# Second MLP products of three chunks as two interleaved groups of seven half-size products, with two of the side sums on GpSimd and six raw weight buffers

## The chip, the cores and the metric

The kernel runs on one core of a Trainium2 chip. The metric is the device time of one execution in microseconds. Before the change the median of 3 runs is 793.33 us (792.94 to 793.57).

## What is computed

One layer of a streaming encoder for 544 tokens (512 prompt frames, 32 sample frames), feature dimension 1024, all float32. The part that matters here is the MLP; its hidden width is 4096 and is worked off in four chunks of 1024:

```python
x = x + merged @ w_out
x = x + jnp.square(jax.nn.relu(rms_norm(x, g_mlp) @ w_up)) @ w_down
x = x + jax.nn.sigmoid(rms_norm(x, g_ple) @ w_ple_gate) * (p[layer] @ w_ple_proj)
```

Before it come the input projection, a pooling mixer and stick-breaking attention, behind it the gate of the last line ("ple") and the final norm. None of these is touched except where they share the weight buffers.

## The kernel before

**Precision.** Every float32 operand is split in a high part (fp32r, made by ScalarE) and a low part (the difference, made by VectorE). A product is three matmuls: high by high, high by low, low by high, each over 272 columns (half the tokens).

**Weights.** Weights come as tiles of 128x1024 (512 KB). SyncE loads a raw tile into one of 10 raw buffers (`RAW_BUFS`, line 84: two in `raw`, eight in `raw_more`), ScalarE makes `w_hi` from it (`hi`, line 699), VectorE makes `w_lo` (`ahead`, line 1456), in a ring of four split tiles (`W_RING`). Both engines make tile t+3 at the step of tile t; ScalarE's `hi` waits until TensorE has finished tile t-1 (semaphore `full`), whose ring place it takes. SyncE fills a raw buffer again when the low part of the tile before in it is made (`wait_free`, line 525; `wlo_done`). It issues strictly in the order of `STAGED_LOADS`.

**First products of a chunk (up).** Each chunk has two groups (g even, g odd; 512 hidden features each). A group is a Winograd form of Strassen's product: seven half-size products in the order A11, S1, S2, S4, S3, A12, A22 of the weight side (`SIDES`, line 71), of 24 matmuls each (`product_of`, line 1352), against seven token-side operands `u_hi`, `u_lo` that lie ready. The weight sides are S1 = A21+A22, S2 = A11+S1, S3 = A21+A11, S4 = A12+S2 in the stored tiles (signs are in the stored weights and operands). Each of the four sums is a second DMA that adds into the raw buffer (`second_part`, line 654, issued by GpSimd, `accum_op=ALU.add`): for S1 and S3 from HBM, for S2 and S4 from another raw buffer. So a group has 7 loads and 4 adding DMAs.

Results accumulate in PSUM (four slots of two banks; an even group has slots 0 and 1, an odd one 2 and 3). ScalarE copies the first three results out to `h_of` (`copy_quarter`, line 933), VectorE adds three more there (`add_quarter`, line 1793) and scales by the inverse norm and clips (`scaled_second`, lines 1817 and 1822; `scaled_first`, line 1803). ScalarE squares (`hidden_hi`, lines 948 and 949) into `b_hi` and in place, VectorE makes `b_lo` (`hidden_lo`, line 1828). `h_of` is single: the next group's first copy waits until the low part of the first half is made.

**Second products of a chunk (down).** Eight dense products of 48 matmuls each (`down`, line 1373, matmuls on lines 1061, 1064 and 1067), from 8 loads, PSUM slots in turn; the first two are interleaved by hidden features so that late features are used last. VectorE adds each result to the residual `xt` (`add_residual`, line 1742). In the last chunk VectorE and ScalarE also build the operands of the ple gate between them.

**GpSimd** only issues the adding DMAs in the MLP. Earlier, in the attention stage, it runs masks (line 634) and the window sums of the pooling mixer (`window_sums`, line 614), while VectorE splits weights (line 1448) and attention operands (lines 1549, 1644).

## Time and profile before

| | |
|---|---|
| median of 3 runs | 793.33 us (792.94 to 793.57) |
| profiled execution | 793.77 us, span 791.9 us |
| granted TensorE clock, mean | 0.996 |
| TensorE busy | 773.7 us (98%) |
| VectorE busy | 494.8 us (62%) |
| ScalarE busy | 381.5 us (48%) |
| GpSimd busy | 96.9 us (12%) |
| DMA moved | 110.18 MB, 139 GB/s mean |
| MLP, from the first up product to the ple gate | 357.99 to 719.98 us of the span |

The span is that of the slowest (here only) core from first to last instruction; the time reported for the same execution is 1.9 us more. PE is TensorE (matmul), PEld its weight load, DVE VectorE, ACT ScalarE, POOL GpSimd, SP SyncE; SPq and POOLq are their DMA issues. Matmuls are pipelined: each is shown as 288 ns long, but successive ones start about 125 ns apart, so busy time and count say more than the mean duration.

### The profile page before, as it was taken

Reading aid. Unit: us, or ns where it says so; the run is one execution under the profiler, and the core shown is the slowest. Engines: PE = TensorE matmul, PEld = TensorE weight load, DVE = VectorE, ACT = ScalarE, POOL = GpSimd, SP = SyncE. Lnnn points to the kernel's source line nnn. Section 1 sums busy time; section 2 is a strip of 40 time slices with the busy share of each in tenths; the row PEclk is TensorE's granted clock in tenths of the full one; section 3 lists DMA queues with packets and bytes.
Section 4 is the critical chain, followed back from the end, with each engine's and each line's share of the span. In section 5 each row is a group of like instructions: output and inputs, shape, how many; then the busy total and the mean of one; then the engine's idle time right before and its main releaser. Section 6 shows DMA issues by size and latency. Waiting matters only on the chain.

```text
span 791.9 us, 14329 instructions
## 1 busy us (share of the span) xinstructions
PE 773.7 (98%) x6050; PEld 765.2 (97%) x6050; DVE 494.8 (62%) x606; ACT 381.5 (48%) x443; POOL 96.9 (12%) x169
## 2 busy tenths in 40 slices
PE   8899999999999999999999999999999999999993
PEld 8899999999999899999999999999999999999993
DVE  5876566566566547787763367434763367677965
ACT  6554534535575443665641255213642155555643
POOL 1040140150150000020001100020001100100001
PEclk9999999999999999999999999999999999999998
DMA  7342231232221316786566847587575856826402
GB/s 236 99 125 74 70 120 53 82 105 56 98 90 55 107 54 206 240 202 178 179 171 168 202 160 206 139 188 183 158 192 145 204 171 180 195 82 161 119 1 113
DMA packets 33097, 110.18 MB, mean 139 GB/s; under 512 B 4496, under 2 KB 4496, under 8 KB 33040
## 3 DMA queue, kind: packets, MB, share of 16 engines
q1 hardware_dynamic: 24768, 84.72, 32.4%
q0 software_dynamic: 6016, 21.04, 14.9%
q10 hardware_dynamic: 2256, 3.60, 1.3%
q8 instruction: 44, 0.72, 0.4%
q14 instruction: 13, 0.11, 0.0%
HBM read 94.33 MB, written 4.52 MB: 125 GB/s over the span
## 4 chain that ended last, share of the span: by engine, by line
PE 90%; DVE 5%; ACT 2%; issue 1%; DMA 1%; SPq 1%; DVEq 0%; ACTq 0%
PE psum L1352 24%; PE psum L1061 19%; PE psum L1067 19%; PE psum L1064 19%; PE psum L1114 1%; DMA xt<-x_t 1%; PE psum L1042 1%; PE psum L1142 1%; PE psum L1043 1%; PE psum L1044 1%; PE psum L1140 1%; PE psum L1430 1%; PE psum L1102 1%; DVE work L1473 1%; PE psum L1101 1%
## 5 line engine op out<-in xcount | busy, mean ns | idle before, releaser
L699 ACT ACTIVATE w_hi<-raw_more 128x1024 fp32r<-128x1024 f32 x84 | 88.7, 1056 | 133.0 <-PE psum L1067 100.7
L1064 PE MATMUL psum<-b_lo,w_hi 128*128 128x272 f32 x688 | 142.0, 288 | 0.0
L1061 PE MATMUL psum<-b_hi,w_hi 128*128 128x272 f32 x672 | 139.3, 288 | 0.0
L1067 PE MATMUL psum<-b_hi,w_lo 128*128 128x272 f32 x672 | 138.8, 288 | 0.0
L1061 PE MATMUL psum<-a_hi,w_hi 128*128 128x272 f32 x576 | 120.8, 291 | 3.3 <-DVE a_lo L1462 1.2
L1456 DVE TENSOR_TENSOR w_lo<-raw_more,w_hi 128x1024 fp32r<-128x1024 f32 x84 | 102.2, 1222 | 34.6 <-ACT w_hi L699 34.3
L1067 PE MATMUL psum<-a_hi,w_lo 128*128 128x272 f32 x576 | 119.0, 288 | 0.0
L1064 PE MATMUL psum<-a_lo,w_hi 128*128 128x272 f32 x576 | 118.8, 288 | 0.0
L1352 PE MATMUL psum<-u_hi,w_hi 128*128 128x272 f32 x560 | 115.9, 288 | 0.2 <-ACT h_of L933 0.2
L1352 PE MATMUL psum<-u_hi,w_lo 128*128 128x272 f32 x560 | 115.7, 288 | 0.0
L1352 PE MATMUL psum<-u_lo,w_hi 128*128 128x272 f32 x560 | 115.5, 287 | 0.0
L1064 PEld LDWEIGHTS psum<-b_lo,w_hi 128*128 128x128 f32 x688 | 108.1, 188 | 0.0
L1061 PEld LDWEIGHTS psum<-b_hi,w_hi 128*128 128x128 f32 x672 | 105.4, 188 | 0.8 <-issue 0.7
L1067 PEld LDWEIGHTS psum<-b_hi,w_lo 128*128 128x128 f32 x672 | 105.1, 189 | 0.0
L1061 PEld LDWEIGHTS psum<-a_hi,w_hi 128*128 128x128 f32 x576 | 90.2, 188 | 4.4 <-DVE a_lo L1462 2.0
L1064 PEld LDWEIGHTS psum<-a_lo,w_hi 128*128 128x128 f32 x576 | 90.5, 189 | 0.0
L1067 PEld LDWEIGHTS psum<-a_hi,w_lo 128*128 128x128 f32 x576 | 90.0, 189 | 0.0
L1352 PEld LDWEIGHTS psum<-u_hi,w_hi 128*128 128x128 f32 x560 | 87.9, 188 | 0.5 <-issue 0.4
L1352 PEld LDWEIGHTS psum<-u_lo,w_hi 128*128 128x128 f32 x560 | 88.3, 188 | 0.0
L1352 PEld LDWEIGHTS psum<-u_hi,w_lo 128*128 128x128 f32 x560 | 87.5, 188 | 0.0
L1742 DVE TENSOR_TENSOR xt<-psum,xt 128x544 f32<-128x544 f32 x40 | 28.9, 723 | 88.2 <-PE psum L1067 88.2
L1448 DVE TENSOR_TENSOR w_lo<-raw,w_hi 128x1024 fp32r<-128x1024 f32 x41 | 51.8, 1265 | 41.5 <-ACT w_hi L691 41.3
(245 smaller groups left out, 1010.3 us busy)
## 6 DMA issues: line engine op xcount, KB each, us to landing
raw_more<-w_tiles SPq DMA_DIRECT2D x84, 512.0 KB, 4.3
raw<-w_tiles SPq DMA_DIRECT2D x66, 512.0 KB, 3.5
raw_more<-w_tiles POOLq DMA_DIRECT2D x16, 512.0 KB, 6.7
raw_more<-raw_more POOLq DMA_DIRECT2D x14, 512.0 KB, 8.3
xt<-x_t SPq DMA_DIRECT2D x8, 272.0 KB, 6.2
y_t<-xt SPq DMA_DIRECT2D x8, 272.0 KB, 2.5
raw<-w_tiles POOLq DMA_DIRECT2D x4, 512.0 KB, 7.6
raw_more<-raw POOLq DMA_DIRECT2D x3, 512.0 KB, 6.4
```

Source lines behind the costliest of these rows:

```text
L699: act.activation(w_hi[:, t % W_RING, :, :].rearrange("p k c -> p (k c)"), src, ACT.Copy)\
L1042: pe.matmul(out, hi, rhi, start=first, stop=False, skip_group_check=True)
L1043: pe.matmul(out, hi, rlo, start=False, stop=False, skip_group_check=True)
L1044: return pe.matmul(out, lo, rhi, start=False, stop=last, skip_group_check=True)
L1061: pe.matmul(base[:, h, :], w_hi[:, s, wk, :], at(hi, k, h * HALF, (h + 1) * HALF), start=(opens and q == 0), stop=False, skip_group_check= ...
L1064: pe.matmul(base[:, h, :], w_hi[:, s, wk, :], at(lo, k, h * HALF, (h + 1) * HALF), start=False, stop=False, skip_group_check=True)
L1067: mm = pe.matmul(base[:, h, :], w_lo[:, s, wk, :], at(hi, k, h * HALF, (h + 1) * HALF), start=False, stop=(closes and q == len(ks) - 1), s ...
L1101: pe.matmul(z, b_lo[:, keys], b_hi[:, both], start=(b != 3), stop=False, skip_group_check=True)
L1352: mm = pe.matmul(out[:, two, :], w_part[:, t % W_RING, 2 * k + two, :], u_part[:, op, k, :], start=(OPENS[s] and k == 0 and w_part is w_hi ...
L1448: dve.tensor_tensor(w_lo[:, s, :, :].rearrange("p k c -> p (k c)"), raw[:, t % RAW_RING, :], w_hi[:, s, :, :].rearrange("p k c -> p (k c)" ...
L1456: dve.tensor_tensor(w_lo[:, t % W_RING, :, :].rearrange("p k c -> p (k c)"), src, w_hi[:, t % W_RING, :, :].rearrange("p k c -> p (k c)"), ...
L1742: dve.tensor_tensor(halves(xt[:, m, :]), slot(n), halves(xt[:, m, :]), ALU.add).then_inc(taken, 1)
```

## The change

In chunks 0, 1 and 2 the second products take the same seven-product form as the first ones. The outputs are split in two sets e = 0, 1 (four of the eight output tiles each), and the 14 products of 24 matmuls run in the order (side, e) = (A11,0), (A11,1), (S1,0), (S1,1), ... The token side is now seven sums of quarters of the hidden features (B11, B21, B22, T3, NT1, NT2, T4), each split in high and low: VectorE makes NT1, T3, NT2 and T4 (`operand_sum`) and all seven low parts (`operand_low`), ScalarE the high parts (`square_hi`, `sum_hi`). They are made by group of hidden features, in the steps around the start of the next group. A product uses hidden features of both groups; for the first two products the part of the even group of both comes first. Chunk 3 stays dense. The first products of all chunks keep their seven products.

In all groups, S2 and S4 are no longer DMAs: GpSimd adds 128x1024 tiles in place, S2 in the buffer of A11 once A11's low part is made, S4 in the buffer of S1 once S1's low part is made. A group has 5 loads and 2 adding DMAs. There are 6 raw buffers in place of 10.

```diff
-LOADS = SIDES
-ADDED = {"S1": ("A21", "A22"), "S2": ("A11", "S1"), "S3": ("A21", "A11"), "S4": ("A12", "S2")}
+LOADS = ("S1", "A11", "A12", "S3", "A22")
+DN_LOADS = ("A11", "S1", "A12", "S3", "A22")
+ADDED = {"S1": ("A21", "A22"), "S3": ("A21", "A11")}
+LIES_IN = {"S2": "A11", "S4": "S1"}
-RAW_BUFS = 10
+RAW_BUFS = 6
```

The order of the loads (`staged_loads`):

```diff
+        if c < SEVENS:
+            seq.extend((DN_GROUPS + 2 * c + e, what) for what in DN_LOADS for e in range(2))
+        else:
+            seq.extend(("down", c, q) for q in range(KT))
```

SyncE, what a load waits for (`wait_free`):

```diff
-                        if what in ("S1", "S2"):
-                            sp.wait_ge((s2_in if what == "S1" else s4_in)[g % 2], 16 * (g // 2 + 1))
-                        sp.wait_ge(wlo_done, t_group(g, SIDES.index(what)) + 1)
+                        if what == "A11":
+                            sp.wait_ge(s4_made, nth_group(g) + 1)
+                        last = {"A11": "S2", "S1": "S4"}.get(what, what)
+                        sp.wait_ge(wlo_done, group_tile(g, last) + 1)
```

GpSimd:

```diff
+            def sum_two(g):
+
+                pool.wait_ge(*side_ready(g, "S1"))
+                pool.wait_ge(wlo_done, group_tile(g, "A11") + 1)
+                a = side_buf(g, "S2")
+                pool.tensor_tensor(a, a, side_buf(g, "S1"), ALU.add).then_inc(s2_made, 1)
+
+            def sum_four(g):
+
+                pool.wait_ge(s2_made, nth_group(g) + 1)
+                pool.wait_ge(*side_ready(g, "A12"))
+                pool.wait_ge(wlo_done, group_tile(g, "S1") + 1)
+                pool.tensor_tensor(side_buf(g, "S4"), side_buf(g, "S2"), side_buf(g, "A12"), ALU.add)\
+                    .then_inc(s4_made, 1)
+
+            def sums_of(g):
+                second_part(g, "S1")
+                second_part(g, "S3")
+                sum_two(g)
+                sum_four(g)
 
             for c in range(CHUNKS):
-                for g, what in ((0, "S1"), (0, "S2"), (1, "S1"), (0, "S4"), (0, "S3"), (1, "S2"), (1, "S3"), (1, "S4")):
-                    second_part(2 * c + g, what)
+                sums_of(2 * c)
+                sums_of(2 * c + 1)
+                if c < SEVENS:
+                    two = (DN_GROUPS + 2 * c, DN_GROUPS + 2 * c + 1)
+                    for g in two:
+                        second_part(g, "S1")
+                    for g in two:
+                        sum_two(g)
+                    for g in two:
+                        sum_four(g)
+                    for g in two:
+                        second_part(g, "S3")
```

ScalarE:

```diff
+            def square_hi(g, name):
+
+                act.activation(two_tiles(operand(0, name, g % 2)), hidden(name), ACT.Square).then_inc(ohi_done, 1)
+                for of in ("B11", "B12") if name == "B11" else (name,):
+                    act.activation(hidden(of), hidden(of), ACT.Square).then_inc(ohi_done, 1)
+
+            def sum_hi(g, name):
+
+                act.wait_ge(sum_done, nth_t(g, name))
+                act.activation(two_tiles(operand(0, name, g % 2)), hidden(name), ACT.Copy).then_inc(ohi_done, 1)
...
+            def up_seven(g):
+
+                for s in range(T_UP):
+                    n = NTH[("up", g, s)]
+                    if s == 0 and g % 2 == 1:
+                        last_quarter_hi(g - 1)
+                        sum_hi(g - 1, "NT1")
+                    ahead(TILE[("up", g, s)])
+                    if s == 0 and g % 2 == 1:
+                        sum_hi(g - 1, "T3")
...
+                    if g and s == 0:
+                        act.wait_ge(olo_done, nth_lo(g - 1, "NT1"))
+                        act.wait_ge(sum_done, nth_t(g - 1, "NT2"))
...
+                    if BY_ACT[s]:
+                        copy_quarter(g, n, s)
```

TensorE:

```diff
+            def down_seven(c):
+
+
+                for from_group in range(2):
+                    for e in range(2):
+                        if from_group == 0:
+                            weights(TILE[("dn", c, 0, e)])
+                            place_for(NTH[("dn", c, 0, e)])
+                        if e == 0:
+                            pe.wait_ge(olo_done, nth_lo(2 * c + from_group, "B11"))
+                        mm = second_product(c, 0, e, from_group)
+                        if from_group == 1:
+                            mm.then_inc(full, 1)
+                for s in range(1, T_UP):
+                    for e in range(2):
+                        weights(TILE[("dn", c, s, e)])
+                        place_for(NTH[("dn", c, s, e)])
+                        if e == 0:
+                            pe.wait_ge(olo_done, nth_lo(2 * c + 1, NAME[OPERAND[s]]))
+                        second_product(c, s, e, 0)
+                        second_product(c, s, e, 1).then_inc(full, 1)
```

VectorE:

```diff
+            def operand_low(g, name):
+
+                dve.wait_ge(ohi_done, nth_hi(g, ("sq " if name[0] == "B" else "hi ") + name))
+                dve.tensor_tensor(two_tiles(operand(1, name, g % 2)), hidden(name),
+                                  two_tiles(operand(0, name, g % 2)), ALU.subtract).then_inc(olo_done, 1)
...
+            def up_seven(g):
+                for s in range(T_UP):
+                    if s == 0 and g % 2 == 1:
+                        scaled_second(g - 1, "A22")
+                        operand_low(g - 1, "B11")
+                        operand_sum(g - 1, "NT1")
+                        operand_low(g - 1, "B21")
+                        operand_sum(g - 1, "T3")
+                        operand_low(g - 1, "NT1")
+                        operand_sum(g - 1, "NT2")
+                    ahead(TILE[("up", g, s)])
+                    if s == 0 and g % 2 == 1:
+                        operand_sum(g - 1, "T4")
+                        operand_low(g - 1, "NT2")
+                        operand_low(g - 1, "T3")
+                    if s == 1 and g % 2 == 1:
+                        operand_low(g - 1, "T4")
+                    if s == 5:
+                        operand_low(g, "B22")
+                    group_step(g, s)
...
+            def down_seven(c):
+                g = 2 * c + 1
+                for j in range(2 * T_UP):
+                    if j == 0:
+                        scaled_second(g, "A22")
+                        operand_low(g, "B11")
+                        operand_sum(g, "NT1")
+                        operand_low(g, "B21")
+                        operand_sum(g, "T3")
+                        operand_low(g, "NT1")
+                        operand_sum(g, "NT2")
+                    ahead(TILE[("dn", c, j // 2, j % 2)])
+                    if j == 0:
+                        operand_sum(g, "T4")
+                        operand_low(g, "NT2")
+                    if j == 1:
+                        operand_low(g, "T3")
+                        operand_low(g, "T4")
+                    second_taken(c, j // 2, j % 2)
```

`group_step` is the old body of `up_group` (`add_quarter`, `scaled_second` of S3, `scaled_first`). `second_taken` adds or subtracts a result in PSUM to or from a quarter of `xt` (544 elements), 14 times in a chunk in place of 8 `add_residual`.

## Rows read from the trace of the kernel before

**Rows 1.** The page, busy time by engine, the whole span.
```profile
PE 773.7 (98%) x6050; PEld 765.2 (97%) x6050; DVE 494.8 (62%) x606; ACT 381.5 (48%) x443; POOL 96.9 (12%) x169
```

**Rows 2.** Windows: one chunk's up part, then its down part; columns in the first line.
```profile
core 0: us, PE busy (x) PEld busy (x) DVE busy (x) ACT busy (x) POOL busy (x), PEclk, DMA share, GB/s
...
449.50:491.60 42.10, 42.10 (x338) 42.10 (x338) 28.67 (x28) 22.69 (x25) 0.87 (x1) 1.00 0.61 180
491.60:539.70 48.10, 48.10 (x386) 48.10 (x385) 18.06 (x19) 11.74 (x12) 6.12 (x7) 1.00 0.70 173
```

**Rows 3.** The chain that ended last, in order of time: start, length, what.
```profile
357.99 9.05 PE psum L1352 x72
...
449.48 42.07 PE psum L1352 x336
539.66 42.05 PE psum L1352 x336
```

**Rows 4.** Groups by line and form, VectorE and ScalarE: count, busy us, mean ns.
```profile
L1742 DVE TENSOR_TENSOR xt<-psum,xt 128x544 f32<-128x544 f32 x40 | 28.9, 723 | 88.2 <-PE psum L1067 88.2
...
L699 ACT ACTIVATE w_hi<-raw_more 128x1024 fp32r<-128x1024 f32 x84 | 88.7, 1056 | 133.0 <-PE psum L1067 100.7 <-PE psum L1352 30.1 <-PE psum L1044 2.1
...
L715 ACT ACTIVATE ev<-xt 128x544 f32<-128x544 f32 x28 | 17.8, 647 | 2.4 <-DVE work L1473 1.0 <-DVE work L1470 0.9 <-issue 0.5
...
L933 ACT ACTIVATE h_of<-psum 128x544 f32<-128x544 f32 x27 | 16.8, 622 | 24.8 <-PE psum L1352 19.0 <-DVE b_lo L1828 5.8
```

**Rows 5.** Timeline where a chunk's up part ends: start, length, instruction [idle before].
```profile
486.41 0.73 DVE L1817 SCALAR_TENSOR_TENSOR h_of<-h_of,rn 128x544 f32<-128x544 f32 x1
487.06 1.22 DVE L1456 TENSOR_TENSOR w_lo<-raw_more,w_hi 128x1024 fp32r<-128x1024 f32 x1
488.66 0.72 DVE L1793 TENSOR_TENSOR h_of<-h_of,psum 128x544 f32<-128x544 f32 x1 [0.38 <-PE psum L1352]
489.41 1.29 DVE L1803 SCALAR_TENSOR_TENSOR h_of<-h_of,rn 128x1088 f32<-128x1088 f32 x1
490.62 1.22 DVE L1456 TENSOR_TENSOR w_lo<-raw,w_hi 128x1024 fp32r<-128x1024 f32 x1
...
491.39 0.41 PE L1061 MATMUL psum<-b_hi,w_hi 128*128 128x272 f32 x2
...
494.10 0.72 DVE L1822 SCALAR_TENSOR_TENSOR h_of<-psum,rn 128x544 f32<-128x544 f32 x1
```

**Rows 6.** Line 1549, its instructions in ns, min/median/max.
```profile
L1549 DVE TENSOR_TENSOR later_lo<-later,later_hi x8: 546/552/1751, 48.8 to 252.0; 128x384 fp32r<-128x384 f32 x8
```

**Rows 7.** Timeline of the attention stage, VectorE beside GpSimd's additions.
```profile
101.11 1.75 DVE L1549 TENSOR_TENSOR later_lo<-later,later_hi 128x384 fp32r<-128x384 f32 x1
101.28 1.16 POOL L614 TENSOR_TENSOR gates<-upad 128x573 f32<-128x573 f32 x1
102.52 1.35 POOL L614 TENSOR_TENSOR gates<-gates 128x571 f32<-128x571 f32 x1
102.79 0.68 DVE L1644 TENSOR_TENSOR b_hi<-psum,b_hi 128x512 fp32r<-128x512 f32 x1
103.39 1.56 DVE L1448 TENSOR_TENSOR w_lo<-raw,w_hi 128x1024 fp32r<-128x1024 f32 x1
```

**Rows 8.** Line 1456, all splits of staged tiles from `raw_more`, ns.
```profile
L1456 DVE TENSOR_TENSOR w_lo<-raw_more,w_hi x84: 1215/1224/1228, 341.8 to 761.5; 128x1024 fp32r<-128x1024 f32 x84
```

**Rows 9.** GpSimd's additions, lines 614 and 625, ns, min/median/max.
```profile
L614 POOL TENSOR_TENSOR gates<-upad x4: 1153/1157/1172, 46.2 to 218.1; 128x573 f32<-128x573 f32 x4
...
L625 POOL TENSOR_TENSOR gates<-gates,invc x4: 185/334/459, 57.4 to 226.0; 128x2 f32<-128x2 f32 x1, 128x4 f32<-128x4 f32 x1, 128x8 f32<-128x8 f32 x1, 128x16 f32<-128x16 f32 x1
```

**Rows 10.** DMA issues: count, KB each, median us to landing; last line: line 663 alone.
```profile
raw_more<-w_tiles SPq DMA_DIRECT2D x84, 512.0 KB, 4.3
...
raw_more<-w_tiles POOLq DMA_DIRECT2D x16, 512.0 KB, 6.7
raw_more<-raw_more POOLq DMA_DIRECT2D x14, 512.0 KB, 8.3
...
DMA to landing us min/median/max: 4.5/7.1/12.4
```

More of the change, by code:

```diff
@@ L1390, in down, with second_product @@
                     dense(slot(n), t % W_RING, ALL, B).then_inc(full, 1)
+            NAME = {B11: "B11", NT1: "NT1", NT2: "NT2", B22: "B22", T3: "T3", B21: "B21", T4: "T4"}
+            def second_product(c, s, e, from_group):
+                t, name = TILE[("dn", c, s, e)], NAME[OPERAND[s]]
+                out = slot(NTH[("dn", c, s, e)])
+                hi, lo = (operand(part, name, from_group) for part in range(2))
+                for i in range(2):
+                    k = 2 * from_group + i
+                    for w_part, h_part in ((w_hi, hi), (w_hi, lo), (w_lo, hi)):
+                        for two in range(2):
+                            mm = pe.matmul(out[:, two, :], w_part[:, t % W_RING, 2 * k + two, :],
+                                           h_part[:, i * HALF:(i + 1) * HALF],
+                                           start=(OPENS[s] and k == 0 and w_part is w_hi and h_part is hi),
+                                           stop=(k == KT // 2 - 1 and w_part is w_lo), skip_group_check=True)
+                return mm
@@ new lines, in operand_sum @@
+            def operand_sum(g, name):
+                first, second = {"NT1": ("B11", "B12"), "T3": ("B22", "B12"), "NT2": ("B22", "NT1"),
+                                 "T4": ("NT2", "B21")}[name]
+                over = {"NT1": "B11", "NT2": "B22", "T4": "B21"}.get(name)
+                if over:
+                    dve.wait_ge(olo_done, nth_lo(g, over))
+                if name == "NT1":
+                    dve.wait_ge(ohi_done, nth_hi(g, "sq B12"))
+                if name != "NT1":
+                    dve.wait_ge(sum_done, nth_t(g, T_ORDER[T_ORDER.index(name) - 1]))
+                if name in ("NT1", "T3"):
+                    ins = dve.tensor_tensor(hidden(name), hidden(first), hidden(second), ALU.subtract)
+                else:
+                    ins = dve.scalar_tensor_tensor(out=hidden(name), in0=hidden(first), scalar=-1.0,
+                                                   in1=hidden(second), op0=ALU.mult, op1=ALU.subtract)
+                ins.then_inc(sum_done, 1)
@@ L1831, in statistics, with second_taken @@
+            def second_taken(c, s, e):
+                n, side = NTH[("dn", c, s, e)], SIDES[s]
+                x = x_quarter(side, e)
+                earlier = {"S4": "S2", "S3": "S1", "A12": "A11"}.get(side)
+                if earlier:
+                    dve.wait_ge(taken, taken_count(NTH[("dn", c, SIDES.index(earlier), e)]))
+                dve.wait_ge(full, n + 1)
+                dve.tensor_tensor(x, x, slot(n), ALU.subtract if X_QUARTER[side][0] else ALU.add).then_inc(taken, 1)
             def statistics(name):
@@ L1886, in _ @@
                 for s in range(T_UP):
-                    ahead(t_ple(g, s))
+                    ahead(TILE[("ple", g, s)])
                     if s == 3 and g == 0:
```

307 lines of the change are left out of this document (202 added, 105 removed).

## The prediction

> **What bounds the kernel now.** The page's busy times come first: TensorE is busy 98% of the span, VectorE 62%, ScalarE 48% [rows 1]. Then the windows: in a chunk TensorE is busy for all 42.10 us of the up part and all 48.10 us of the down part at full granted clock, while VectorE works 28.67 and 18.06 us [rows 2]. The chain in order of time says the same: a chunk's 336 up matmuls are one unbroken piece of 42.07 us, and the next chunk's piece starts 90.18 us after the last one's [rows 3]. So a matmul costs 42.07/336 = 0.1252 us, and 720 of them are 90.15 us: a chunk is TensorE's work and nothing else. Fewer matmuls shorten it as long as VectorE, ScalarE, GpSimd and the loads keep inside it.
>
> **What goes.** A down part falls from 8x48 = 384 to 14x24 = 336 matmuls: 48x0.1252 = 6.01 us a chunk, **18.0 us** for three. The new chunk is 84.1 us of matmuls, and a product lasts 3.005 us. The bound from below is thus 793.8 - 18.0 = 775.8.
>
> **What comes, and its price.** VectorE: a split 1.22 us [rows 8], an operation on 544 elements 0.72 [rows 4], `scaled_first` 1.29. In the timeline the next operation starts 0.08 us before the last one's end if it doesn't need its result (489.41 to 490.62 for one of 1.29), else 0.03 after it (488.66 to 489.41 for 0.72) [rows 5]. So I count 1.14 or 1.25, 0.64 or 0.75, 1.21. ScalarE: a split 1.06, 544 elements 0.65 from SBUF and 0.62 from PSUM [rows 4]. A chunk's VectorE work becomes 28 splits, 14 `second_taken`, and twice 16 operations on 544 and a `scaled_first`: 28x1.22 + 46x0.72 + 2x1.29 = 70 us of 84. It fits, but not evenly: the operands of a group fall within 15 us around the start of the next one.
>
> GpSimd's sums: no row shows one of 1024 elements. A 573-element addition takes 1.15 us and a two-element one 0.185 [rows 9]: by slope 1.93, by proportion 2.06. I take 1.9. The Trainium skill, GPSIMD Engine Reference, "Performance versus the Vector engine", gives 4497 ns for 2048 float32, so about 2.25 us here as an estimate; by that the result would be about 5 us later than below. No run here shows it yet.
>
> The **lock** matters more. While GpSimd adds, a VectorE instruction with both inputs in SBUF stands still: `later_lo`, 384 elements, has a median of 0.552 us and once 1.751 [rows 6]; that one starts at 101.11, GpSimd's addition ends at 102.44, and it ends 0.42 later. Then GpSimd's second addition lasts 1.35 instead of 1.15, and the split behind it 1.56 instead of 1.22; yet line 1644, with one input in PSUM, takes 0.68 in the midst [rows 7]. Today's MLP has nothing of this: its 84 splits lie between 1215 and 1228 ns [rows 8], though GpSimd issues adding DMAs there. The change puts 8 sums into a chunk, 15 us of lock, and splits, low parts, operand sums and `scaled_first` all have two SBUF inputs; `add_quarter`, `second_taken` and the scaling of A22 don't. Bounds: 0 if the sums fall into VectorE's pauses, 1.9 each if not.
>
> **Even to odd up group.** Time 0 is the start of the odd group. S2's sum waits for the low part of A11, made at step 4: -6.3 to -4.4; the scaling of S3 waits for it, and the split of step 5 runs -3.76 to -2.54. That was S1, so S4's sum starts, -2.5 to -0.6. Low B22 -0.6, add 0.04, `scaled_first` 0.8, split 2.0, A22 3.1, low B11 3.8, NT1 4.5, low B21 5.2, T3 5.9, low NT1 6.5, NT2 7.25 to 7.97. Only then may ScalarE copy the new group's first result (it overwrites B11 and NT1): done at 8.6. TensorE needs that PSUM place for its third product at 6.01: a stall of **2.6 us**. Should VectorE win the race for low B22 it is 2.0. With no lock the same list, begun with low B22 at -2.98, ends the copy at 6.3: 0.3.
>
> **Odd group to down.** Time 0 is the first down product. The loads of S1 for down wait for the odd group's tiles 3 and 5; by the order of work above their low parts are made 14.6 and 9.5 us before time 0, and a load of 4.3 and an addition of 6.7 us [rows 10] end at -3.3 and 1.6. So the sums of S2 want to run then. VectorE's split of step 5 ends -3.05; S2 for e=0 -3.05 to -1.15; low B22, add, `scaled_first` at 0.25, split 1.46 to 2.68; S2 for e=1 2.68 to 4.58. A22 leaves PSUM slot 2 at 3.32, which the second down product needs at 1.50: 1.85 lost. Low B11 ends 5.3 (0.5 lost). S4 for e=0 5.3 to 7.2. NT1, B21, T3 and low NT1 end 9.84, needed at 8.35: 1.55 lost. NT2, split to 11.7, T4; S4 for e=1 12.4 to 14.3; low NT2, a result taken, and the split of tile 4 ends 16.8, needed at 15.9: 0.9 lost. Sum **4.8**.
>
> **The six buffers.** S3 for e=0 is loaded over S2 when tile 4's low part is made: 16.8 + 4.3 + 6.7 + 2.4 for both splits = 30.2; TensorE wants it at 19.8 + 9.0 = 28.8. That costs **1.4**. Without the locks VectorE makes tile 4 at 9.9, so 23.3 against 24.04: hidden. The additions range from 4.5 to 12.4 us, median 7.1, and those between raw buffers have 8.3 [rows 10]: 8.3 would add 1.6 a chunk, so 5 in all. The other loads have slack: the next group's S1 is loaded once tile 10's low part is made, some 10 us before it is needed. The fewer bytes save nothing, since nothing waits for bandwidth [rows 2].
>
> **The sum.** A chunk: -6.01 + 2.6 + 4.8 + 1.4 = +2.8; three: +8.4. In chunk 0 the even group's statistics already delay the kernel before (its period is 91.5, from 357.99 to 449.48 [rows 3], 1.3 over TensorE's work), and the two delays partly coincide: 0.4 less. In chunk 3 the same two sums cost VectorE 3.8 us but the first copy, done at about 5.4, is still ahead of 6.01: nothing. The ple gate's sums fall among 6-us products: nothing, and up to 1.5 if they meet its operands. 793.77 + 8.0 = 801.8 against the profiled execution, which lies 0.44 over the median: **801.4**.
>
> **The rivals.** (1) The locks cost nothing, because the sums fall into VectorE's pauses or beside its PSUM operations: stalls 0.3 + 0.1 a chunk, 793.3 - 3x5.6 = **776.5**, faster. For it: VectorE has 14 us a chunk to spare. Against it: the sums are released by low parts that VectorE makes at just those steps, and the same pair of operations did collide in the attention stage [rows 7]. It decides once the stalls are under 6.01 a chunk. 0.15. (2) Half the locks bite, races go VectorE's way: stalls 2.0 + 2.5 + 0.3, 793.3 - 3x1.2 = **789.7**. 0.17. (3) The adding DMAs and the buffers become the bound, as two that follow one another take 8.3 to 12 us: 1.6 to 5 us a chunk more than forecast, 806 to 816, say **811**. 0.18. (4) The matmuls don't shrink: excluded by the count, 336 a down part. The forecast, from 796 to 806, has 0.50.
>
> **How the numbers follow.** A change within 0.2%, 1.6 us, is about what a measurement of this kernel can't tell from none. Rivals 1 and 2 hold 0.32, of which 0.04 lies within it, and 0.02 of the forecast does: faster 0.28, same 0.06, slower 0.66. The range goes from 779 to 812: it leaves out half or more of rival 1 and the top of rival 3. The forecast's own range is 796 to 806.
>
> **What would show it.** In the windows a chunk of about 93 us with TensorE busy 84. GpSimd's additions at 1.9 to 2.3 us, longer where VectorE holds the lock. Splits, until now 1228 ns at most, with maxima near 3.1 us, while line 1742's successor stays at 0.72. TensorE idle before the third product of an odd group, released by ScalarE's copy, and in the first six down products, released by VectorE. If splits keep to 1.22 us, the lock theory is wrong, and the time should be near 777. If TensorE's long waits end on `w_hi` with a DMA behind it, it is rival 3.

## The result and the profile after

The changed kernel takes **839.87 us** (median of 4 runs, 838.80 to 842.29) against 793.13 (792.93 to 793.57, 4 runs) on the same chip: 1.059 times the time, 95% interval 1.057 to 1.062. The forecast was 801.4, and no case that I named reached 840. The profiled execution has a span of 837.7 us against 791.9, so 45.8 us are to be found. The page of the changed kernel, busy time by engine [rows 1]:

```profile
PE 778.2 (93%) x5906; PEld 765.7 (91%) x5906; DVE 602.0 (72%) x696; ACT 414.0 (49%) x503; POOL 173.6 (21%) x193
```

The 144 matmuls are gone (6050 to 5906), which is 18.0 us, yet TensorE is *more* busy: 778.2 us instead of 773.7. And it stands still for 59.5 us of the span instead of 18.2. So the ledger has three lines: -18.0 for the matmuls, +41.3 of idle time, and +22.5 of busy time that the same matmuls did not cost before (778.2 less 773.7 - 18.0). The third line has no counterpart in the prediction.

Windows of chunk 1, up part and down part; the columns are those of [rows 2], and these two lines answer to the two there:

```profile
461.99:513.00 51.01, 47.06 (x348) 46.68 (x349) 41.28 (x41) 27.15 (x37) 14.87 (x9) 0.93 0.54 145
513.00:563.99 50.99, 43.51 (x324) 42.48 (x325) 36.25 (x37) 17.81 (x20) 13.79 (x9) 0.97 0.52 145
```

The chunk takes 102.0 us instead of 90.2. Its 672 matmuls are 84.1 us at the old spacing; TensorE shows 90.6 busy and 11.4 idle, and the granted clock, 1.00 before, is now 0.93 and 0.97.

**Where TensorE waits.** The timeline of TensorE in the changed kernel, only its lines with idle time in front (in brackets: us, and what ended it). These are all from the first up product to the ple gate:

```profile
389.90 0.79 PE L1534 MATMUL psum<-u_hi,w_hi 128*128 128x272 f32 x2 [4.58 <-ACT h_of L1051]
412.53 0.79 PE L1585 MATMUL psum<-b_hi,w_hi 128*128 128x272 f32 x2 [3.84 <-DVE h_of L2046]
438.80 0.52 PE L1585 MATMUL psum<-b_hi,w_hi 128*128 128x272 f32 x2 [0.83 <-DVE w_lo L1680]
442.68 0.52 PE L1585 MATMUL psum<-b_hi,w_hi 128*128 128x272 f32 x2 [0.60 <-DVE w_lo L1680]
461.99 0.49 PE L1534 MATMUL psum<-u_hi,w_hi 128*128 128x272 f32 x2 [4.00 <-DVE xt L2089]
493.29 0.67 PE L1534 MATMUL psum<-u_hi,w_hi 128*128 128x272 f32 x2 [2.51 <-ACT h_of L1051]
513.00 0.49 PE L1585 MATMUL psum<-b_hi,w_hi 128*128 128x272 f32 x2 [1.44 <-DVE h_of L2046]
515.10 0.52 PE L1585 MATMUL psum<-b_hi,w_hi 128*128 128x272 f32 x2 [0.35 <-DVE b_lo L2060]
519.93 0.37 PE L1585 MATMUL psum<-t_more,w_hi 128*128 128x272 f32 x1 [1.56 <-DVE ev_r L2060]
540.82 0.52 PE L1585 MATMUL psum<-b_hi,w_hi 128*128 128x272 f32 x2 [2.23 <-DVE w_lo L1680]
563.99 0.49 PE L1534 MATMUL psum<-u_hi,w_hi 128*128 128x272 f32 x2 [3.32 <-DVE xt L2089]
595.29 0.49 PE L1534 MATMUL psum<-u_hi,w_hi 128*128 128x272 f32 x2 [2.51 <-ACT h_of L1051]
615.01 0.49 PE L1585 MATMUL psum<-b_hi,w_hi 128*128 128x272 f32 x2 [1.42 <-DVE h_of L2046]
617.11 0.52 PE L1585 MATMUL psum<-b_hi,w_hi 128*128 128x272 f32 x2 [0.36 <-DVE b_lo L2060]
621.94 0.49 PE L1585 MATMUL psum<-t_more,w_hi 128*128 128x272 f32 x2 [1.56 <-DVE ev_r L2060]
628.89 0.52 PE L1585 MATMUL psum<-t_more,w_hi 128*128 128x272 f32 x2 [0.66 <-DVE w_lo L1680]
644.26 0.82 PE L1585 MATMUL psum<-b_hi,w_hi 128*128 128x272 f32 x2 [3.02 <-DVE w_lo L1680]
667.84 0.79 PE L1534 MATMUL psum<-u_hi,w_hi 128*128 128x272 f32 x2 [2.48 <-DVE xt L2089]
701.10 0.49 PE L1534 MATMUL psum<-u_hi,w_hi 128*128 128x272 f32 x2 [1.61 <-ACT h_of L1051]
792.36 0.49 PE L1534 MATMUL psum<-u_hi,w_hi 128*128 128x272 f32 x2 [2.60 <-DVE h_of L2185]
```

Read by releaser, this is the prediction's list and three entries that it had at nothing. Sums over the three chunks in us, forecast beside measured:

| place | released by | forecast | measured |
|---|---|---|---|
| third product of the odd group | ScalarE's copy, L1051 | 7.4 | 9.6, of which 0.2 were there before |
| first six down products | VectorE, L2046, L2060, split | 14.4 | 11.2 |
| down tiles 8 and 9 (S3) | split behind two DMAs | 4.2 | 6.7 |
| first product of the next chunk | `second_taken`, L2089 | 0 | **9.8** |
| chunk 3, third product | ScalarE's copy | 0 | 1.6 |
| ple gate, second group | VectorE, L2185 | 0 | 2.6 |

**The lock.** Two lines of the changed kernel's timeline, some 10 us in front of the wait that ends at 595.29:

```profile
584.64 2.95 POOL L765 TENSOR_TENSOR raw_more<-raw 128x1024 f32<-128x1024 f32 x1 [1.89 <-DVE w_lo L1680]
...
586.00 2.74 DVE L2027 SCALAR_TENSOR_TENSOR h_of<-h_of,rn 128x1088 f32<-128x1088 f32 x1
```

`scaled_first` takes 2.74 us instead of its own 1.29, and GpSimd's sum runs until 587.59, 1.15 before its end. By line, in ns, min/median/max: the splits (which answer to [rows 8]), the 42 additions from PSUM, and GpSimd's commonest form of a sum [rows 9]:

```profile
L1680 DVE TENSOR_TENSOR w_lo<-raw_more,w_hi x84: 1211/1221/3064, 340.5 to 807.3; 128x1024 fp32r<-128x1024 f32 x84
...
L2089 DVE TENSOR_TENSOR xt<-xt,psum x42: 706/714/724, 420.5 to 670.6; 128x544 f32<-128x544 f32 x42
...
L758 POOL TENSOR_TENSOR raw_more<-raw_more x8: 2338/2460/3149, 341.9 to 785.3; 128x1024 f32<-128x1024 f32 x8
```

With an input in PSUM nothing is held up: the additions of 420.49 and 522.75 lie wholly within a sum and take 0.72 and 0.71 us. The splits, both inputs in SBUF, reach 3.06 (3.39 among those from `raw`). A sum is 2.34 us when nothing holds it up and up to 3.15 in this form, 3.38 in any, when VectorE does; I had 1.9. The Trainium skill's figure (GPSIMD Engine Reference, "Performance versus the Vector engine") gave 2.25 as an estimate, and the measurement lies just above it, so the page was nearer than my slope.

**The wait before the next chunk.** Chain in order of time of the changed kernel, behind tile 10's split (down tile j = 10), start, length, what:

```profile
648.74 1.14 DVE w_lo L1680
649.90 3.50 DMA raw_more<-w_tiles
653.69 9.84 DMA raw_more<-w_tiles
663.55 1.07 ACT w_hi L817
664.65 2.42 DVE w_lo L1680
667.07 0.64 DVE xt L2089
667.84 16.66 PE psum L1534 x120
```

With six buffers the next group's S1 can be loaded only once tile 10's low part is made. Load, adding DMA and `w_hi` take until 664.6; the adding DMA alone took 9.84 us where I took 6.7. While it ran the core's DMA engines were full: their busy share over 653.69 to 663.53 is 1.03, and 0.86 to 1.02 over the other four adding DMAs on such chains; the chunk's means of 0.54 and 0.52 don't show it. TensorE needs that tile only for the second product of the chunk, 3 us later than the first. But VectorE's queue has its split *ahead of* `second_taken`, the operation that frees the PSUM slot for the next chunk's first product. So the late tile stops TensorE a product early, and the lock of S2's sum (663.60 to 665.98) makes that split 2.42 us long.

**The clock.** Windows of 2 us around the wait that ends at 595.29; the columns again as in [rows 2], the granted clock third from the end:

```profile
592.00:594.00 2.00, 0.79 (x7) 0.57 (x5) 2.00 (x4) 2.00 (x3) 0.00 (x0) 1.00 0.00 0
594.00:596.00 2.00, 0.70 (x5) 0.74 (x6) 2.00 (x3) 1.56 (x4) 0.00 (x0) 0.95 0.01 4
596.00:598.00 2.00, 2.00 (x11) 2.00 (x11) 2.00 (x4) 2.00 (x4) 0.00 (x0) 0.50 0.51 170
598.00:600.00 2.00, 2.00 (x13) 2.00 (x13) 2.00 (x3) 0.65 (x1) 0.00 (x0) 0.69 0.89 352
600.00:602.00 2.00, 2.00 (x18) 2.00 (x17) 0.61 (x2) 1.57 (x2) 0.88 (x1) 1.00 0.24 37
```

TensorE is fully busy from 596 but shows 11 matmuls in 2 us instead of the 18 of the last line: it runs at 1.2 instead of 2.4 GHz. From the granted clocks of 0.95, 0.50 and 0.69 that is some 3.4 us. The same is found behind ten of the twenty waits, every one of 2.23 us or more. Busy time times (1 - granted clock), summed over all 2-us windows from 340 us to the end of the second ple group's recovery, is 19.6 us (the kernel before: 0.0 from 340 to 738). The remaining 3 of the 22.5 I take for tails: the last matmul ahead of a wait is counted to its end instead of to the next one's start. At the 0.3 us a wait measured below, twenty of them would be 6, so the parts for clock and tails are sure only to some 3 us.

### The profile page after: what moved, and what is told of

It is laid out like the page before. It is cut to its first block, busy times and chain, and to the rows that moved or that the text cites. A ratio compares the mean times of both kernels' runs of the same rounds, so it can differ in the third digit from the quotient of the medians.

```text
span 837.7 us, 14286 instructions
## 1 busy us (share of the span) xinstructions
PE 778.2 (93%) x5906; PEld 765.7 (91%) x5906; DVE 602.0 (72%) x696; ACT 414.0 (49%) x503; POOL 173.6 (21%) x193
## 3 DMA queue, kind: packets, MB, share of 16 engines
q1 hardware_dynamic: 22752, 77.38, 27.3%
q0 software_dynamic: 4864, 16.84, 11.4%
## 4 chain that ended last, share of the span: by engine, by line
PE 59%; DVE 19%; DMA 11%; issue 5%; ACT 4%; SPq 1%; POOL 1%; DVEq 0%; ACTq 0%; POOLq 0%
PE psum L1534 15%; PE psum L1243 12%; PE psum L1249 12%; PE psum L1246 12%; DMA raw_more<-w_tiles 7%; DVE w_lo L1680 4%; DMA raw<-w_tiles 3%; DVE h_of L2027 2%; DVE b_lo L2060 2%; DVE h_of L2075 1%; PE psum L1296 1%; DVE h_of L2017 1%; DVE h_of L2041 1%; ACT w_hi L817 1%; DVE xt L2089 1%
## 5 line engine op out<-in xcount | busy, mean ns | idle before, releaser
L1680 DVE TENSOR_TENSOR w_lo<-raw_more,w_hi 128x1024 fp32r<-128x1024 f32 x84 | 111.0, 1325 | 51.8 <-ACT w_hi L817 51.4
L1534 PE MATMUL psum<-u_hi,w_hi 128*128 128x272 f32 x560 | 121.1, 299 | 23.6 <-ACT h_of L1051 11.2
L1534 PEld LDWEIGHTS psum<-u_hi,w_hi 128*128 128x128 f32 x560 | 92.6, 198 | 25.3 <-DVE w_lo L1680 13.2
L1243 PEld LDWEIGHTS psum<-a_hi,w_hi 128*128 128x128 f32 x576 | 90.2, 188 | 4.5 <-DVE a_lo L1686 2.0
L1672 DVE TENSOR_TENSOR w_lo<-raw,w_hi 128x1024 fp32r<-128x1024 f32 x41 | 52.0, 1267 | 41.4 <-ACT w_hi L809 41.2
L1680 DVE TENSOR_TENSOR w_lo<-raw,w_hi 128x1024 fp32r<-128x1024 f32 x43 | 57.4, 1335 | 29.8 <-ACT w_hi L817 27.5
L750 POOL DMA_DIRECT2D raw_more<-w_tiles x22 | 19.2, 874 | 237.3 <-DMA raw_more<-w_tiles 237.3
L1246 PE MATMUL psum<-b_lo,w_hi 128*128 128x272 f32 x304 | 62.8, 288 | 0.0
L817 ACT ACTIVATE w_hi<-raw 128x1024 fp32r<-128x1024 f32 x38 | 40.0, 1055 | 42.6 <-DMA raw<-w_tiles 21.0
L726 POOL TENSOR_SCALAR_AFFINE_SELECT work<-work 128x128 f32<-128x128 f32 x64 | 20.6, 357 | 192.7 <-DVE work L1756 114.7
L1243 PE MATMUL psum<-b_hi,w_hi 128*128 128x272 f32 x288 | 59.9, 290 | 0.0
L1249 PE MATMUL psum<-b_hi,w_lo 128*128 128x272 f32 x288 | 59.3, 287 | 0.0
```

What stands on the lines that cost most here:

```text
L726: pool.affine_select(out=d, in_=d, compare_op=ALU.is_gt, fill=0.0, base=0, pattern=[[1, P]], channel_multiplier=-1).then_inc(done, 1)
L750: pool.dma_start(raw_buf(n), w_tiles[quarter_tile(g, ADDED[what][1]), :, :], accum_op=ALU.add)\
L817: act.activation(w_hi[:, t % W_RING, :, :].rearrange("p k c -> p (k c)"), src, ACT.Copy)\
L1243: pe.matmul(base[:, h, :], w_hi[:, s, wk, :], at(hi, k, h * HALF, (h + 1) * HALF), start=(opens and q == 0), stop=False, skip_group_check= ...
L1246: pe.matmul(base[:, h, :], w_hi[:, s, wk, :], at(lo, k, h * HALF, (h + 1) * HALF), start=False, stop=False, skip_group_check=True)
L1249: mm = pe.matmul(base[:, h, :], w_lo[:, s, wk, :], at(hi, k, h * HALF, (h + 1) * HALF), start=False, stop=(closes and q == len(ks) - 1), s ...
```

## The experiments

### Which part costs: the sums or the adding DMAs

Three kernels, each cutting the work of one operation but leaving every instruction and every wait in place. They leave out most of the side sums.

```diff
-                pool.tensor_tensor(a, a, side_buf(g, "S1"), ALU.add).then_inc(s2_made, 1)
+                pool.tensor_tensor(a[:, 0:16], a[:, 0:16], side_buf(g, "S1")[:, 0:16], ALU.add).then_inc(s2_made, 1)
...
-                pool.dma_start(raw_buf(n), w_tiles[quarter_tile(g, ADDED[what][1]), :, :], accum_op=ALU.add)\
+                pool.dma_start(raw_buf(n)[:, 0:64], w_tiles[quarter_tile(g, ADDED[what][1]), :, 0:64], accum_op=ALU.add)\
```

Short sums (the first edit, in S4 too):

> GpSimd's sums S2 and S4 add only 16 of 1024 columns (the rest of S2 and S4 is left unsummed), with all waits as they are. Lock theory (GpSimd's sums hold VectorE up where the operands of a group are made): the waits at the start of the odd group and of down (6.5 us in chunks 1 and 2) fall under 1 us, so does the slow clock behind the first, and tile 4 is split earlier, so the loads lose most of their lateness too: 785 to 797 us. Buffer theory (six buffers and adding DMAs of 9 to 10 us set the pace): the waits before tile 8 and before the next chunk stay, 815 to 830 us.

Short adding DMAs (the second edit alone):

> The adding DMAs of S1 and S3 carry 64 of 1024 columns (the rest of S1 and S3 lacks its second part), GpSimd's sums stay whole. Lock theory: the waits at the group starts stay at 6 us or more a chunk with the slow clock behind the longest; the waits before tile 8 (3.0 us) and before the next chunk (2.5 to 3.3) go: 808 to 820 us. Buffer theory: under 800 us.

Both:

> Both edits at once: only 16 columns summed and 64 added. Both theories together: nothing is left to wait for, 776 to 782 us (793.8 less 18.0 us of matmuls, plus 0 to 6 us of what VectorE loses at the group starts by its own work). If it stays over 790, VectorE's and ScalarE's new operand work by itself costs the rest.

| | median us | ratio to before |
|---|---|---|
| changed kernel | 839.87 | 1.059 (1.057 to 1.062) |
| short sums | 799.97 | 1.008 (1.005 to 1.011) |
| short adding DMAs | 810.51 | 1.022 (1.016 to 1.028) |
| both short | 777.33 | 0.980 (0.977 to 0.983) |

Each lies at or near its theory's range. Short sums are 3 us over it: waits of 1.78, 1.45 and 0.75 us stay at the start of down, where I had expected less than 1, and they are gone when the DMAs are short too. The 62.5 us between the first and the last row are the sums and the DMAs, and nothing else: with both short, TensorE has one wait of 1.38 us (third product of chunk 0's odd group, 0.17 in the kernel before, so it comes with the new operands' work) and a mean granted clock of 0.996. The sums by themselves cost 810.5 - 777.3 = 33.2, the DMAs 800.0 - 777.3 = 22.6, and together they cost 6.7 more than that. With short sums the splits have their own length again, all of them (line 1680, ns):

```profile
L1680 DVE TENSOR_TENSOR w_lo<-raw_more,w_hi x84: 1209/1220/1228, 341.3 to 768.2; 128x1024 fp32r<-128x1024 f32 x84
```

Ten waits remain there, 16.2 us in all. The three longest lie where the chain above put them, before a chunk:

```profile
450.96 0.49 PE L1534 MATMUL psum<-u_hi,w_hi 128*128 128x272 f32 x2 [2.57 <-DVE xt L2089]
...
542.18 0.49 PE L1534 MATMUL psum<-u_hi,w_hi 128*128 128x272 f32 x2 [2.42 <-DVE xt L2089]
...
633.75 0.79 PE L1534 MATMUL psum<-u_hi,w_hi 128*128 128x272 f32 x2 [3.29 <-DVE xt L2089]
```

**Is it the lock, or only that the sum is late?** Short sums, with four clearings of a scratch strip ahead of each: GpSimd is busy nearly as long, but reads nothing.

```diff
+                for k in range(4):
+                    link(pool.memset(scratch[:, :], 0.0))
```

> As e1_short_sums (16 of 1024 columns summed), but ahead of each short sum GpSimd writes four times 512 zeros to a scratch area, which reads nothing and takes about the 2.4 us that a whole sum took. It tells the lock from the mere lateness of S2 and S4. Lock theory (what costs is that GpSimd reads SBUF while VectorE wants two inputs from it): as e1, 797 to 805 us, and VectorE's splits keep to about 1.23 us. Lateness theory (the tiles come 2.4 us later, and GpSimd's queue is held): over 820 us.

802.36 us, 1.012 (1.009 to 1.014): 2.4 over short sums, little beside the 37.5 that are left to the changed kernel. A clearing took 0.53 us, so each sum came 2.1 us later; the splits kept between 1209 and 1242 ns. So what costs in a real sum is the stopped VectorE and not the late result. The Trainium skill (SBUF — State Buffer, "Who interferes with whom") says that a VectorE instruction with two SBUF inputs is held up by a GpSimd instruction that reads SBUF and not by one that only writes; this pair of kernels agrees.

### The sums without the down products

`SEVENS = 0`, with what follows from it: the GpSimd sums and the six buffers stay, chunks 0 to 2 have dense down products again.

> One part alone: six buffers and GpSimd's sums as in the changed kernel, but all second products dense as before (8 of 48 matmuls). Lock theory: two sums a group meet VectorE where it has 3 us to spare, and only the ple gate's wait of 2.6 us with a slow clock of 2 us behind it comes on top: 793 to 800 us. Buffer theory: six buffers delay the dense tiles as well: over 803 us.

806.36 us, 1.017 (1.014 to 1.020), above the 793 to 800 that I gave the lock. It has six waits, 10.8 us in all. Five lie at the start of an odd group, 1.60 to 1.73 us each, and are the lock's: in each up part GpSimd's S4 holds `scaled_first`, and the copy behind is late (timeline, chunk 1):

```profile
472.31 2.40 POOL L765 TENSOR_TENSOR raw<-raw_more 128x1024 f32<-128x1024 f32 x1 [1.89 <-DVE w_lo L1687]
472.81 3.05 DVE L2034 SCALAR_TENSOR_TENSOR h_of<-h_of,rn 128x1088 f32<-128x1088 f32 x1
...
485.06 0.49 PE L1541 MATMUL psum<-u_hi,w_hi 128*128 128x272 f32 x2 [1.60 <-ACT h_of L1051]
```

The sixth, 2.60 us in the ple gate, is not the lock's but that of GpSimd's queue (below, "GpSimd's order in the ple gate"): its chain has the same 8.9 us in which GpSimd stands on a load. No up or down tile is late, so the six buffers alone cost nothing in the chunks; that rival falls there. My error was to say that this place had 3 us to spare.

### Other ways to make the sums

S2 by an adding DMA from the other raw buffer, as in the kernel before:

```diff
-                pool.tensor_tensor(a, a, side_buf(g, "S1"), ALU.add).then_inc(s2_made, 1)
+                pool.dma_start(a, side_buf(g, "S1"), accum_op=ALU.add).then_inc(s2_in[nth_group(g) % 2], 16)
```

> S2 is summed by an adding DMA from the buffer of S1 instead of by GpSimd; S4 stays on GpSimd. Half the locks go, but S2 comes 7 to 10 us after its summands instead of 2.4, and GpSimd's queue stands on it before S4. Lock theory, if the lateness fits: 820 to 832 us. If the lateness of S2 in the down parts takes its place (its summand S1 is ready only 0 to 3 us after the down part starts, and the split of tile 4 is due at 9): over 838 us.

844.24 us, 1.065 (1.058 to 1.072), not distinguishable from the changed kernel. The first down products wait less (0.16, 0.75 and 0.65 us in chunk 1), but now tiles are late: 5.06 and 4.91 us before third products, where VectorE's queue stood on a split behind an adding DMA (7.49 us for the first), and 9.15 in the ple gate.

Both sums on VectorE, right behind S1's split (GpSimd keeps only the DMAs):

```diff
+                if t >= T_MLP and t < N_TILES and name[0] in ("up", "dn", "ple") and SIDES[name[2]] == "S1":
...
+                    sum_two(g)
+                    sum_four(g)
```

> Both sums of a group are made by VectorE behind the split of S1 instead of by GpSimd; nothing else is changed. A sum costs VectorE 1.22 us of work instead of up to 2.4 us behind the lock. Lock theory: the up-to-up wait stays near 2.5 us (2.4 us of work for 2.4 of lock), the down part's first waits shrink by 3 to 4 us a chunk: 818 to 832 us. If GpSimd's latency or its queue were the cause rather than VectorE's time, the first waits would go altogether and it would fall under 812 us.

837.11 us (834.5 and 839.7), above my range; two executions can't tell it from the changed kernel. There is no lock left (the longest split is 1.23 us), the waits at the start of down are 2.36 in all instead of 3.35 (chunk 1), but now the sums too stand ahead of `second_taken` in VectorE's queue, and the next chunk waits 5.39, 5.15 and 6.37. With six buffers neither way made the kernel clearly faster.

### The order of the queues

Tile 8's wait: only the down groups' S3 adding DMA is short (64 columns; it leaves out the rest of those sums).

> The adding DMA of S3 in the down parts alone carries 64 of 1024 columns (S3's second part is left out there for the rest); S1's stay whole. If the wait before the next chunk is only the child of S3's lateness (tile 10 is split late, so the next S1 is loaded late), both waits go, with the slow clock behind them: 808 to 816 us. If S1's own chain of load and addition is too long for six buffers, the wait before the next chunk stays at 2 us or more: 822 to 832 us.

829.49 us, 1.046 (1.042 to 1.049). The waits before tile 8 are gone, but those before a chunk stay, 2.11, 3.03 and 4.68: the chain of the next S1 is by itself too long for six buffers, here 3.40 + 10.47 us for its two DMAs (from 638.02). No run had more buffers, so what a seventh would give is not shown.

VectorE's order: in the last two down steps `second_taken` goes ahead of the split.

```diff
+                    if j >= 2 * T_UP - 2:
+                        second_taken(c, j // 2, j % 2)
                     ahead(TILE[("dn", c, j // 2, j % 2)])
```

> In the last two steps of a down part VectorE adds the finished result to the residual before it splits the next weight tile, instead of behind it. If TensorE's wait before the next chunk (4.0, 3.3 and 2.5 us) is that of PSUM slot 0 behind a VectorE queue which stands on the split of S1, it shrinks by 1 us or more each, with part of the slow clock behind it: 828 to 836 us. If S1's arrival alone sets it, it stays: 838 to 842 us.

831.81 us (828.3 and 835.4). The first product of a chunk now waits 1.34, 0.32 and 1.01 us instead of 4.00, 3.32 and 2.48. The median is 8 lower, but two executions so far apart don't show by how much; the one whose waits are given here (835.4) gained 4. Part of it comes back: the third product of the odd group waits 3.94 instead of 2.51, the start of down 4.03 instead of 3.35 (chunk 1).

GpSimd's order in the ple gate. There the S3 adding DMA of the second group stood ahead of S2's sum in GpSimd's queue and waited for a load whose buffer was not free; the changed kernel's chain shows 8.72 us of it:

```profile
775.94 8.72 issue
784.69 0.86 POOL raw L750
785.55 2.49 POOL raw_more L758
788.07 1.07 ACT w_hi L817
```

```diff
+            sums_of(PLE_GROUPS)
+            second_part(PLE_GROUPS + 1, "S1")
+            sum_two(PLE_GROUPS + 1)
+            sum_four(PLE_GROUPS + 1)
+            second_part(PLE_GROUPS + 1, "S3")
```

> Only the ple gate's second group changed: GpSimd issues S3's adding DMA behind the two sums instead of ahead of them. If the wait of 2.6 us there comes from GpSimd's queue, which stands on the load of S3 while S2's summands lie ready, it goes, with the slow clock behind it: 834 to 837 us. If it comes from S1's adding DMA, nothing changes: 839 to 841 us.

836.14 us, 1.054 (1.051 to 1.057): 3.7 less, just at the edge of the two intervals, with waits of 1.77 and 0.46 us in place of the 2.60 and its slow clock.

Both orders together:

> The changed kernel, whole, with both of the orders that helped by themselves: the sums of the second ple group ahead of its S3 adding DMA, and second_taken ahead of the split in the last two down steps. The two waits lie in different stages, so the gains should add: 3.7 + 8.1 us off 839.9, 828 us, between 824 and 832. If the lateness that one gives back is only taken up behind (a rival: VectorE's backlog sets the end, whatever the order), it stays over 832. Either way it stays above the kernel before (793).

832.43 us (829.5 to 835.6), 1.049 (1.046 to 1.051): clearly less than the changed kernel, but no better than the VectorE order alone was and over the 828 to which the gains would have added up. Waits of 5.32 and 4.16 us in chunk 1 (in the execution of 835.6) took the place of those removed. VectorE's backlog passes on what an order gives. That no order of these two reaches the kernel before is shown; that none could is not.

### What a wait costs with its clock

Idle matmuls put into the long waits (their number first too high, then sized to the wait; 128 columns, result not used):

> The changed kernel whole, with idle matmuls of 128 columns into unused PSUM columns ahead of the ten long waits of TensorE, each train shorter than the wait (0.5 to 3.8 us in all at 56 ns each), so that TensorE isn't idle. Clock theory (22.5 us of the loss are matmuls at the lower granted clock behind the waits): granted clock 0.985 or more, 817 to 828 us. Rival (the slow matmuls lie beside VectorE's backlog, which sets the end anyway): 836 to 842 us.

848.04 us, 1.069 (1.066 to 1.072). Inconclusive: such a matmul takes 0.11 us at full clock (a train of 32 lasts 3.69) and 0.21 behind a wait (20 in 4.17) instead of the 0.06 that I had sized by, and the trains outlasted the waits.

> The changed kernel whole, with idle matmuls of 128 columns that accumulate into unused PSUM columns ahead of TensorE's long waits, now counted at the 0.21 us that one took in e6_fillers, so that each train ends shortly before the wait does; the train before the next chunk stands at its first product, where the wait is. Clock theory (22.5 us of the loss are matmuls at the lower granted clock): granted clock 0.99 or more, 818 to 828 us. Rival (they lie beside VectorE's backlog, which sets the end anyway): 835 to 842 us.

835.91 us, 1.054 (1.050 to 1.059): 4 us less where the theory had 12 to 22. It doesn't decide either, since the clock still fell, for two reasons. A train could start only once its own PSUM slot was free, so waits remained ahead of some, as here:

```profile
540.05 1.83 PE L1530 MATMUL psum<-negone 128*128 128x128 f32 x8 [3.65 <-DVE xt L2106]
```

And I had sized the trains by 0.21 us a matmul, so those at full clock lasted about half as long as meant:

```profile
592.09 1.22 PE L1530 MATMUL psum<-negone 128*128 128x128 f32 x10
594.75 0.69 PE L1543 MATMUL psum<-u_hi,w_hi 128*128 128x272 f32 x2 [1.44 <-ACT h_of L1051]
```

Behind such a train the clock fell after idle times of 1.21, 1.44 and 1.66 us, and did not after others of 1.43 and 1.66.

So the price was measured by itself. The kernel with both shortened has no long wait. In its last down stage three waits were put on TensorE, before products 3, 5 and 7, each for 2, 4 or 6 clearings by GpSimd (like the shortened kernel these three leave out most of the sums):

```diff
+            def probe(q):
+                pool.wait_ge(full, NTH[("down", CHUNKS - 1, q - 1)] + 1)
+                for k in range(4):
+                    ins = pool.memset(scratch[:, :], 0.0)
...
+                    if q in (3, 5, 7):
+                        pe.wait_ge(gone, (q - 1) // 2)
```

> The kernel with short sums and short adding DMAs (777.3 us, no long wait left), with three waits put on TensorE in the last down stage, before products 3, 5 and 7: each waits for GpSimd to clear a scratch strip twice after the product before has ended (2 x 0.6 us and the signals, some 1.5 us a wait). Nothing else waits for anything but TensorE there. Theory, the granted clock falls only behind waits of over 2 us: the time grows by the waits alone, 3 x 1.5, to 781.8 us, and the products behind them last 6.01 us as the others. Rival, each wait costs clock, whatever its length: the products behind last 8 us or more and the time is 788 or over.

> The same with four clearings, some 2.6 us a wait. Theory: behind each wait the granted clock is 0.5 for 4 to 6 us, so the matmuls there last 2 to 3 us longer; 777.3 + 3 x 2.6 + 3 x 2.5 = 792.6 us, of which half is clock. Rival, the slow clock in the changed kernel has another cause (few matmuls over a longer stretch, heat) and follows no single wait: 777.3 + 7.8 = 785.1 us with products of 6.01 us behind the waits.

> The same with six clearings, idle times of some 3.6 us. Of three idle times of 2.48 us one was followed by a granted clock of 0.50 to 0.71 for 3 us (about 1.5 us lost) and two by 1.00; of 1.32 us none. Theory: at 3.6 us all three are followed by the lower clock, for 3 to 6 us: 777.3 + 3 x (3.6 + 0.35) + 3 x 1.5 to 2.5 = 793.7 to 796.7 us. Rival, it is chance and not the length of the wait that decides, one in three or none: 789 to 791.

| idle time of each | median us | over 777.33 | per wait | slow stretches |
|---|---|---|---|---|
| 1.32 us | 782.17 | 4.8 | 1.6 | none |
| 2.48 us | 787.13 | 9.8 | 3.3 | one of three |
| 3.64 us | 793.97 | 16.6 | 5.5 | three of three |

The first and the last came as the theory said. The middle one fell between the theory and its rival, since behind only one of its three waits the clock fell: 2.48 us lies where it can go either way. Nor is it the same in each execution: three took 787.0 to 787.1 at a mean granted clock of 0.993, the fourth 789.72 at 0.989. A wait costs its idle time and 0.3 us (the tail). Then 3 x (3.64 + 0.3) = 11.8, and 4.8 more for three slow stretches: **1.6 us each**. With 2.48 the same sum leaves 1.5 for one stretch. Windows of the middle wait in the kernel with 3.64, as above:

```profile
692.00:694.00 2.00, 0.00 (x0) 0.00 (x0) 1.58 (x4) 1.10 (x2) 1.83 (x4) 1.00 0.00 0
694.00:696.00 2.00, 1.04 (x7) 1.08 (x8) 1.49 (x3) 1.21 (x2) 0.93 (x3) 0.91 0.04 8
696.00:698.00 2.00, 2.00 (x11) 2.00 (x10) 0.00 (x0) 0.00 (x0) 0.00 (x0) 0.50 0.00 0
698.00:700.00 2.00, 2.00 (x14) 2.00 (x14) 0.00 (x0) 0.00 (x0) 0.00 (x0) 0.73 0.00 0
```

VectorE and ScalarE are idle there from 696 on: nothing but the clock makes TensorE slow. That it follows single waits, and longer ones more surely, is shown by none, one and three of three. This fits the ledger: ten stretches of the changed kernel at 1.6 are 16 of the 19.6 us read from its windows, and three of the ten cost more (2.3, 2.9 and 3.1 us, behind waits of 4.58, 3.84 and 3.02).

## Why the prediction was wrong, by its steps

- **What goes.** 18.0 us: right. With sums and DMAs shortened the kernel takes 777.3, against a bound from below of 775.8; its one wait of 1.38, 0.17 in the kernel before, is most of the rest.
- **The lock, even to odd group.** The mechanism is right; that the size is right to the tenth, 2.6 forecast and 2.51 twice, is luck. The copy was forecast for 8.6 us after the odd group's start. The wait of 2.51 puts it near 8.4. Two errors cancelled: the sum is longer than I took, so `scaled_first` ended 2.0 us after that start instead of 0.8, and the operations behind it took less than I counted. In chunk 0 the wait was 4.58 in place of 0.17; I had counted 2.2 there. I had read the 1.3 us of chunk 0's longer period before as delay that would partly coincide, but TensorE stood still for only 0.17 of them; the rest was busy time, with four matmuls of the statistics (at 366.9 to 367.9) in it.
- **Odd group to down.** 4.8 forecast, 3.35 and 4.00 in chunks 1 and 2. In chunk 0 it was 3.84, in one wait. The mechanism holds, the single terms are smaller.
- **The adding DMAs.** Mis-sized: I took 6.7 us, the median [rows 10], and "nothing waits for bandwidth" from a chunk's mean share [rows 2]. On the chain they took 9.06 to 10.00 us (median of line 750 now 7.7), with the DMA engines 0.86 to 1.03 busy in those stretches: the mean over a chunk hides that they are full just where an adding DMA is waited for. That the plain loads beside it lengthen it fits; no run took them away. Tiles 8 and 9 cost 6.7 us of waits instead of 4.2.
- **"The other loads have slack: ... some 10 us before it is needed."** This step failed in kind. It compares the load with the time at which *TensorE* needs the tile. But VectorE's queue has that tile's split ahead of `second_taken`, so the tile is needed a product earlier, and the chain to it is 3.5 + 9.84 + 1.1 + 2.4 us. It cost 9.8 us of waits.
- **The ple gate, "nothing, and up to 1.5".** 2.6 and a slow stretch. I looked for the sums' lock on the operands, not for what stands ahead of a sum in GpSimd's own queue.
- **Chunk 3, "nothing".** 1.6: `scaled_first` was held up there as in the other chunks, and the copy was not done at 5.4.
- **No step at all for the clock.** Of the 63.8 us that stand against the 18.0, 19.6 are TensorE at the lower granted clock behind waits that I had counted at their idle time alone. My own forecast had waits of 2.6 us, so by the price measured here even it would have been a few us short.
- **The rivals.** The locks are not free (rival 1: 33 us by themselves). Rival 3, DMAs and buffers as the bound, had the right direction but is not the cause alone: with the sums short, 7.0 us over the kernel before remain.

In sum the waits that I worked out came to 26.0 us and measured 27.3 (27.5 less the 0.2 that was there before), so close because single terms were off both ways: +2.0 at the third products (9.4 new), -3.2 at the first down products, +2.5 at tiles 8 and 9. The other 36.5 of the 63.8 us are two queues read from the wrong end (9.8 + 2.6), chunk 3 (1.6), the clock (19.6) and what I take for tails (2.9).

## What to carry to other kernels

Ask of a late tile not when its user needs it, but what stands behind its next instruction in that engine's queue: a split that waits for a DMA also holds back the operation that frees a PSUM slot. Price a wait of TensorE of some two microseconds or more with what it can cost behind its end, here 1.6 us and up to 3.1. Read the DMA engines' share in the stretch where a transfer is waited for, not as a mean over the stage. A sum moved from the DMA queues to GpSimd is paid for by VectorE, while GpSimd reads, and so belongs only where VectorE's work has an input in PSUM or there is none.

## What was not expected of the hardware

- The granted clock falls behind single waits that are short. With three equal waits it fell behind none of 1.32 us, one of three of 2.48 and all of 3.64. Over the kernels here without idle matmuls, from the first up product on: behind none of up to 1.73 us, behind 28 of the 42 between 1.77 and 2.71, behind all 46 of 2.76 or more. Waits of 1.77 and of 2.51 us occur with and without it; what decides there stays open.
- The price of such a fall, by the windows, is 1.3 to 1.7 us in 53 of the 74; the other 21, all behind waits of 3.02 us or more, cost 2.2 to 3.1.
- Adding DMAs of 512 KB on the chains took 9.06 to 10.47 us each, though the load ahead of them took 3.4 to 3.6; the DMA engines were 0.86 to 1.03 busy meanwhile.
- An fp32r matmul of 128 columns, weights and data the same tile, is hardly cheaper than one of 272: in a train they follow one another 0.11 us apart (32 in 3.69 us), against 0.125.
